# Feed-forward layer with seven block products for gate and up, and the weights' block sums on GpSimd

## The chip, the cores and the metric

The kernel runs on one core of a Trainium2 chip. The metric is the time of one execution on the device in microseconds (us); several executions are timed and their median is taken. The trace comes from one more execution, taken by the hardware profiler.

The engines in the text: TensorE (PE, with its weight loads PEld), VectorE (DVE), ScalarE (ACT), GpSimd (POOL) and SyncE (SP, which issues the loads).

## The reference

One inference step of a hybrid decoder layer for 512 prompt rows and 8 sample rows, so 520 columns in the transposed layout that the kernel uses. What matters here is the last step before the final norm, the feed-forward layer:

```
D_MODEL = 2048
D_FF = ((8 * D_MODEL + 3 * 256 - 1) // (3 * 256)) * 256

def channel_mix(x, lw):
    h = rms_norm(x, lw['g_ffn'])
    return x + (jax.nn.silu(h @ lw['w_gate']) * (h @ lw['w_up'])) @ lw['w_down']
```

D_FF is 5632. Everything is float32.

## The kernel before

The kernel is a sequence of stages (norm, input projection, RWKV, attention branches, output projection, feed-forward, final norm). Each stage is one block with an instruction list for each engine; the engines meet only at semaphores, and within one engine the instructions run in the order written. The change is in `stage_ffn`.

The residual `g.xt` lies in SBUF as 16 tiles of 128 x 520 (2048 features by 520 columns). The moving operands are halves of 260 columns (`HC`), each with a PSUM bank of its own. To reach float32 accuracy each product is made three times in the fast fp32r form: an operand is split into a rounded high part and the low remainder, and `three_products` adds high x high, high x low and low x high.

The loop runs over 11 rounds (`PARTS`), each for 512 of the 5632 hidden features. A round takes 12 weight tiles of 128 x 2048 (1 MB) in turn: gate and up for each of 4 hidden tiles, then 4 for the down projection. For tile n:

- SP loads it into one of 3 slots of `w_raw` (`load`, L2676 and L2680), when the tile that used the slot is finished;
- ScalarE rounds it to `w_hi` (`high`, L2751), VectorE subtracts to `w_lo` (`low`, L2779), both two tiles ahead of TensorE;
- TensorE multiplies: 16 x 6 = 96 matmuls of 260 columns for each gate or up tile, 4 x 2 x 2 x 6 = 96 for each down tile;
- VectorE scales the gate by the norm's factor (`gate`, L2785), ScalarE applies the Silu (L2760), GpSimd scales again (L2702), VectorE multiplies by up (`hidden`, L2791) and splits the result (L2793, L2795); for the down projection it adds the PSUM banks to the residual (`add`, L2803).

Norm: the factor 1/sqrt(mean square) of each column is not multiplied into the input but into gate and up afterwards, so that TensorE can begin as soon as the first input tile is scaled by the gain (ScalarE, L2764) and split (VectorE, L2823).

A line of `three_products` stands for matmuls of several stages; in the rows `d_ps<-hh` are gate and up, `d_ps<-f_hid_hi` is down. `three_products` is also used by the compression stage (`m_ps`), there with one output bank at a time. Rows of the RWKV preparation (`r_...`) show GpSimd and VectorE at work together.

Of the kernel before, what the change touches and what calls it, by code (L numbers as in the profile page):

```python
# [15 lines left out]
F32 = mybir.dt.float32  # L16
# [2132 lines left out]
def stage_nsa_prompt(nc, g):  # L2149
# [9 lines left out]
    with ExitStack() as ctx:  # L2159
# [28 lines left out]
        adr_in, late_in = sem("adr_in"), sem("late_in")  # L2188
# [310 lines left out]
def stage_out_proj(nc, g):  # L2499
    HC = TC // 2  # L2500
    with ExitStack() as ctx:
# [13 lines left out]
        with nc.Block() as block:  # L2515
# [10 lines left out]
            @block.gpsimd  # L2526
            def _(pool):
                for q in range(4, 8):
                    pool.wait_ge(mix_lo, q - 3)
                    mix_load(pool, g, q)  # L2530
# [101 lines left out]
def stage_ffn(nc, g):  # L2632
    HC = TC // 2
    HT = 4
    PARTS = D_FF // P // HT
    UN = 3 * HT
    SUMS = 16
    GR = 12
    assert PARTS * HT * P == D_FF and D == 2048
    with ExitStack() as ctx:  # L2640
        w_raw = g.wo_raw.rearrange("p s k n -> p s (k n)")
        w_hi = ctx.enter_context(nc.sbuf_tensor("f_w_hi", [P, 3, 2048], F32R))
        w_lo = ctx.enter_context(nc.sbuf_tensor("f_w_lo", [P, 3, 2048], F32R))
        hid_hi = ctx.enter_context(nc.sbuf_tensor("f_hid_hi", [P, HT, TC], F32R))
        hid_lo = ctx.enter_context(nc.sbuf_tensor("f_hid_lo", [P, HT, TC], F32R))
        spare = g.mix_raw.rearrange("p a b (h t) -> p a b h t", h=2)
        sg, act_up, rstd = spare[:, 0], spare[:, 1, 0], spare[:, 2]
        gain = ctx.enter_context(nc.sbuf_tensor("f_gain", [P, KT], F32))
        ps = g.ps_d
        loaded = [new_sem(nc, g, f"f_w_in{i}") for i in range(3)]  # L2650
        gain_in = new_sem(nc, g, "f_gain_in")
        hi_done, lo_done, summed, freed = (new_sem(nc, g, "f_" + n) for n in ("hi_done", "lo_done", "summed", "freed"))
        h_hi, h_lo, root_ready, rstd_ready = (new_sem(nc, g, "f_" + n) for n in ("h_hi", "h_lo", "root_ready", "rstd_ready"))
        gate_ready, silu_ready, gated, hid_split, hid_ready = (new_sem(nc, g, "f_" + n) for n in (
            "gate_ready", "silu_ready", "gated", "hid_split", "hid_ready"))
# [4 lines left out]
        def through(n):  # L2660

            return n + 1 if n < 2 * HT else 2 * HT + 2 * (n - 2 * HT) + 2

        def both(t):
            return t.rearrange("p (h t) -> p h t", h=2)

        with nc.Block() as block:
            @block.sync
            def _(sp):
                def load(i, n):  # L2670

                    i, n = (i, n) if n < UN else (i + 1, n - UN)
                    w = w_raw[:, n % 3, :]
                    if n < 2 * HT:
                        src = (gate_v, up_v)[n % 2][:, :, bass.ds(i * (HT * P) + (n // 2) * P, P)]
                        sp.dma_start(w.rearrange("p (k n) -> p k n", k=KT), src).then_inc(loaded[n % 3], 16)  # L2676
                    else:
                        v = n - 2 * HT
                        src = down_v[:, bass.ds(i * HT, HT), v * 512:(v + 1) * 512]
                        sp.dma_start(w.rearrange("p (k n) -> p k n", k=HT), src).then_inc(loaded[n % 3], 16)  # L2680

                def part(i, last):
                    for n in range(UN - 3 if last else UN):
                        sp.wait_ge(summed, i * SUMS + through(n))
                        load(i, n + 3)
                with nc.allow_non_contiguous_dma(reason="one value to a partition"):
                    sp.dma_start(gain[:], g.g_ffn.rearrange("(k p) -> p k", p=P)).then_inc(gain_in, 16)
                for n in range(3):
                    load(0, n)
                with sp.Fori(0, PARTS - 1) as i:  # L2690
                    part(i, False)
                part(PARTS - 1, True)

            @block.gpsimd
            def _(pool):
                clear_old(pool, g)
                pool.wait_ge(rstd_ready, 1)
                with pool.Fori(0, PARTS) as i:
                    for j in range(HT):
                        pool.wait_ge(silu_ready, i * HT + j + 1)  # L2700
                        take_wait(g, pool)
                        pool.tensor_tensor(sg[:, j % 2], sg[:, j % 2], rstd[:, 1], ALU.mult).then_inc(gated, 1)  # L2702

            @block.tensor
            def _(pe):
                def bank(group, j):
                    return ps[:, 4 * (group % 2) + j, 0:HC]

                def halves(x, k):
                    return [x[:, k, h * HC:(h + 1) * HC] for h in range(2)]  # L2710

                def part(i, first):
                    for n in range(2 * HT):
                        j, m, s = n // 2, n % 2, n % 3
                        pe.wait_ge(lo_done, i * UN + n + 1)
                        if m == 0:

                            pe.wait_ge(freed, i * GR + j + 1)
                        for k in range(KT):
                            if first and n == 0:  # L2720
                                pe.wait_ge(h_lo, k + 1)
                            cols = slice(k * P, (k + 1) * P)
                            last = three_products(pe, [bank(j, 2 * m + h) for h in range(2)], w_hi[:, s, cols], w_lo[:, s, cols],
                                                  halves(g.hh, k), halves(g.hl, k), k == 0, k == KT - 1)
                        last.then_inc(summed, 1)
                    for v in range(HT):
                        s = (2 * HT + v) % 3
                        pe.wait_ge(lo_done, i * UN + 2 * HT + v + 1)
                        for pair in range(2):
                            group = HT + 2 * v + pair  # L2730
                            pe.wait_ge(freed, i * GR + group + 1)

                            for ks in (range(HT - 1), range(HT - 1, HT)):
                                for m in range(2):
                                    for k in ks:
                                        if v + pair + m == 0:
                                            pe.wait_ge(hid_ready, i * HT + k + 1)
                                        c = k * 512 + (2 * pair + m) * P
                                        last = three_products(pe, [bank(group, 2 * m + h) for h in range(2)],
                                                              w_hi[:, s, c:c + P], w_lo[:, s, c:c + P],  # L2740
                                                              halves(hid_hi, k), halves(hid_lo, k), k == 0, k == HT - 1)
                            last.then_inc(summed, 1)
                for i in range(PARTS):
                    part(i, i == 0)

            @block.scalar
            def _(act):
                def high(i, n):
                    s = n % 3
                    act.wait_ge(loaded[s], i * (16 * UN // 3) + (n // 3 + 1) * 16)  # L2750
                    act.copy(w_hi[:, s, :], w_raw[:, s, :]).then_inc(hi_done, 1)  # L2751

                def part(i, last):
                    for n in range(UN):
                        if not last or n + 2 < UN:
                            high(i, n + 2)
                        if n < 2 * HT and n % 2 == 0:
                            j = n // 2
                            act.wait_ge(gate_ready, i * HT + j + 1)
                            act.activation(sg[:, j % 2], sg[:, j % 2], ACT.Silu).then_inc(silu_ready, 1)  # L2760

                act.wait_ge(gain_in, 16)
                for k in range(KT):
                    act.activation(g.hh[:, k, :], g.xt[:, k, :], ACT.Copy, scale=gain[:, k:k + 1]).then_inc(h_hi, 1)  # L2764
                    if k == 3:
                        high(0, 0)
                act.wait_ge(freed, 2)
                act.activation(rstd[:, 0], rstd[:, 0], ACT.Sqrt).then_inc(root_ready, 1)
                high(0, 1)
                with act.Fori(0, PARTS - 1) as i:  # L2770
# [4 lines left out]
            def _(dve):  # L2775
                def low(i, n):
                    s = n % 3
                    dve.wait_ge(hi_done, i * UN + n + 1)
                    dve.tensor_tensor(w_lo[:, s, :], w_raw[:, s, :], w_hi[:, s, :].bitcast(F32),  # L2779
                                      ALU.subtract).then_inc(lo_done, 1)  # L2780

                def gate(i, j):
                    dve.wait_ge(summed, i * SUMS + 2 * j + 1)
# [380 lines left out]
```

## Time and profile before

| | |
|---|---|
| median of 3 runs | 3720.39 us (3712.27 to 3722.6) |
| profiled execution | 3726.19 us, span 3724.6 us |
| TensorE's granted clock, mean | 0.939 |
| feed-forward stage | about 2158 to 3690 us of the span |
| weights loaded by the stage | 132 loads of 1 MB |
| matmuls of the stage | 12672 (8448 for gate and up, 4224 for down) |

The span runs from the first to the last instruction; the execution's time is a little more. A group of rows gives the line, engine, operation, out<-in, the shapes and the count; then busy time and the mean of one in ns; then the idle time of the engine just before them and what ended it. The matmuls are pipelined: one lasts 283 ns in the rows, but the next starts long before it ends.

### The profile page before, as it was taken

Reading aid. Unit: us, or ns where it says so; the run is one execution under the profiler, and the core shown is the slowest. Engines: PE = TensorE matmul, PEld = TensorE weight load, DVE = VectorE, ACT = ScalarE, POOL = GpSimd, SP = SyncE. Lnnn points to the kernel's source line nnn. Section 1 sums busy time; section 2 is a strip of 40 time slices with the busy share of each in tenths; the row PEclk is TensorE's granted clock in tenths of the full one; section 3 lists DMA queues with packets and bytes.
Section 4 is the critical chain, followed back from the end, with each engine's and each line's share of the span. In section 5 each row is a group of like instructions: output and inputs, shape, how many; then the busy total and the mean of one; then the engine's idle time right before and its main releaser. Section 6 shows DMA issues by size and latency. Waiting matters only on the chain. (4 is left out here: it accounts for less than half of the span.)

```text
span 3724.6 us, 67944 instructions
## 1 busy us (share of the span) xinstructions
PE 3379.1 (91%) x29423; PEld 3102.5 (83%) x29423; DVE 1407.2 (38%) x1761; ACT 1015.3 (27%) x1402; POOL 578.7 (16%) x697
## 2 busy tenths in 40 slices
PE   6999996769859999678779989999999999999997
PEld 6999996458837777454439989999999999999997
DVE  3222221833345665146633243333333333333334
ACT  4111111623215665134402132222122122122112
POOL 2000000534514333362000000000000000000000
PEclk8999998679979999769989999999999999999999
DMA  7433333455525442464143233233333233333332
GB/s 212 114 114 112 109 87 109 152 159 143 142 85 228 180 191 91 140 177 94 37 170 100 70 91 91 91 91 91 91 91 91 91 91 91 93 94 95 94 92 92
DMA packets 490816, 426.40 MB, mean 114 GB/s; under 512 B 124725, under 2 KB 439590, under 8 KB 485918
## 3 DMA queue, kind: packets, MB, share of 16 engines
q1 hardware_dynamic: 468222, 300.40, 28.8%
q0 software_dynamic: 20736, 122.13, 9.3%
q8 instruction: 214, 3.51, 0.4%
q14 instruction: 44, 0.36, 0.0%
q10 hardware_dynamic: 1600, 0.01, 0.0%
HBM read 382.99 MB, written 66.78 MB: 121 GB/s over the span
## 5 line engine op out<-in xcount | busy, mean ns | idle before, releaser
L2779 DVE TENSOR_TENSOR f_w_lo<-wo_raw,f_w_hi 128x2048 fp32r<-128x2048 f32 x132 | 302.5, 2292 | 813.1 <-ACT f_w_hi L2751 813.1
L53 PE MATMUL d_ps<-hh,f_w_hi 128*128 128x260 f32 x2816 | 567.6, 283 | 11.3 <-DVE f_w_lo L2779 11.3
L57 PE MATMUL d_ps<-hh,f_w_lo 128*128 128x260 f32 x2816 | 568.2, 283 | 0.0
L55 PE MATMUL d_ps<-hl,f_w_hi 128*128 128x260 f32 x2816 | 567.3, 283 | 0.0
L2751 ACT CAST f_w_hi<-wo_raw 128x2048 fp32r<-128x2048 f32 x132 | 252.1, 1910 | 998.1 <-DMA wo_raw<-in_w_gate 400.7
L53 PEld LDWEIGHTS d_ps<-hh,f_w_hi 128*128 128x128 f32 x2816 | 435.1, 189 | 11.9 <-DVE f_w_lo L2779 11.8
L57 PEld LDWEIGHTS d_ps<-hh,f_w_lo 128*128 128x128 f32 x2816 | 434.9, 189 | 0.0
L55 PEld LDWEIGHTS d_ps<-hl,f_w_hi 128*128 128x128 f32 x2816 | 433.6, 189 | 0.0
L53 PE MATMUL p_ps<-xh,p_w_hi 128*128 128x264 f32 (+2 forms) x1504 | 306.8, 285 | 10.8 <-DVE p_w_lo L306 10.8
L2702 POOL TENSOR_TENSOR mix_raw<-mix_raw 128x520 f32<-128x520 f32 x44 | 57.4, 1306 | 1621.7 <-ACT mix_raw L2760 1621.7
L55 PE MATMUL p_ps<-xl,p_w_hi 128*128 128x264 f32 (+2 forms) x1504 | 306.3, 285 | 0.0
L57 PE MATMUL p_ps<-xh,p_w_lo 128*128 128x264 f32 (+2 forms) x1504 | 305.6, 285 | 0.0
L53 PE MATMUL d_ps<-f_hid_hi,f_w_hi 128*128 128x260 f32 x1408 | 283.7, 283 | 1.2 <-DVE xt L2803 1.2
L57 PE MATMUL d_ps<-f_hid_hi,f_w_lo 128*128 128x260 f32 x1408 | 283.4, 283 | 0.0
L55 PE MATMUL d_ps<-f_hid_lo,f_w_hi 128*128 128x260 f32 x1408 | 282.4, 282 | 0.0
L53 PEld LDWEIGHTS p_ps<-xh,p_w_hi 128*128 128x128 f32 (+1 forms) x1504 | 232.8, 188 | 11.2 <-DVE p_w_lo L306 10.9
L55 PEld LDWEIGHTS p_ps<-xl,p_w_hi 128*128 128x128 f32 (+1 forms) x1504 | 232.9, 188 | 0.0
L57 PEld LDWEIGHTS p_ps<-xh,p_w_lo 128*128 128x128 f32 (+1 forms) x1504 | 232.6, 188 | 0.0
L1632 DVE TENSOR_TENSOR m_tb_lo<-m_ps,m_tb_hi 128x512 fp32r<-128x512 f32 (+1 forms) x272 | 169.2, 662 | 155.8 <-ACT m_tb_hi L1565 154.1
L53 PEld LDWEIGHTS d_ps<-f_hid_hi,f_w_hi 128*128 128x128 f32 x1408 | 217.6, 188 | 2.1 <-issue 1.9
L55 PEld LDWEIGHTS d_ps<-f_hid_lo,f_w_hi 128*128 128x128 f32 x1408 | 216.3, 188 | 0.0
L57 PEld LDWEIGHTS d_ps<-f_hid_hi,f_w_lo 128*128 128x128 f32 x1408 | 216.1, 188 | 0.0
(456 smaller groups left out, 5054.2 us busy)
## 6 DMA issues: line engine op xcount, KB each, us to landing
p_w<-in_w_in SPq DMA_DIRECT2D x46, 1024.0 KB, 5.6
wo_raw<-in_w_gate SPq DMA_DIRECT2D x44, 1024.0 KB, 5.6
wo_raw<-in_w_up SPq DMA_DIRECT2D x44, 1024.0 KB, 5.6
wo_raw<-in_w_down SPq DMA_DIRECT2D x44, 1024.0 KB, 5.1
wo_raw<-in_w_o SPq DMA_DIRECT2D x16, 1024.0 KB, 6.0
rk_chunks<-r_outb POOLq DMA_DIRECT2D x8, 1280.0 KB, 6.2
s_cur<-rk_chunks SPq DMA_DIRECT2D x8, 1280.0 KB, 7.2
s_one_vecs<-samp_rows SPq DMA_DIRECT2D x80, 128.0 KB, 4.7
```

The costliest lines, as they stand in the source:

```text
L53: pe.matmul(out[j], w_hi, x_hi[j], start=start, stop=False)
L55: pe.matmul(out[j], w_hi, x_lo[j], start=False, stop=False)
L57: last = pe.matmul(out[j], w_lo, x_hi[j], start=False, stop=stop)
L1632: dve.tensor_tensor(tb_lo[:, n % 4, 0:4 * w], ps[:, n % 4, 0:4 * w], tb_hi[:, n % 4, 0:4 * w].bitcast(F32), ALU.subtract).then_inc(dve_ev, 1)
L2702: pool.tensor_tensor(sg[:, j % 2], sg[:, j % 2], rstd[:, 1], ALU.mult).then_inc(gated, 1)
L2751: act.copy(w_hi[:, s, :], w_raw[:, s, :]).then_inc(hi_done, 1)
L2779: dve.tensor_tensor(w_lo[:, s, :], w_raw[:, s, :], w_hi[:, s, :].bitcast(F32), ALU.subtract).then_inc(lo_done, 1)
```

## The change

Gate and up are each computed by a Strassen-Winograd scheme with seven block products in place of eight. A round now makes 256 hidden features (22 rounds). The input is cut into 2 x 2 blocks (feature half by column half), the weights of a round likewise (feature half by hidden tile), each weight block 128 x 1024. The products are made in the order A11, S2, S3, S1, A12, S4, A22 (numbers 0 to 6 of gate, 7 to 13 of up), with

- S1 = A21 + A22, S2 = S1 - A11, S3 = A11 - A21, S4 = A12 - S2 of the weight blocks, made by GpSimd in every round (by VectorE only before the first gate);
- the like sums of the input blocks, made and split once before the loop (`t_f`, `t_hi`, `t_lo`), with the norm's factor and the gain multiplied in first;
- the four result quadrants put together by VectorE from the PSUM banks (`quarters`).

Each product is 8 x 3 = 24 matmuls into one bank. The down projection is 4 units of 48 matmuls a round (numbers 14 to 17), with two outputs of 24 each.

Weight loads are 512 KB, into six slots of `raw`; A21 lies in slot 1 and becomes S3 in place, and the low part also overwrites its raw block in place. Slots 0, 1, 4 and 5 serve the down projection too. So the low part of A11 waits until S3 has been made, and that of S2 until S4 has. The old weight and mixing buffers are released before the stage, and GpSimd clears one more list of semaphores at the start of the output projection.

The core of the diff (new lines of `stage_ffn`):

```diff
-    HT = 4
-    PARTS = D_FF // P // HT
-    UN = 3 * HT
...
+    KH = KT // 2
+    PARTS = D_FF // P // 2
+    PC = 7
+    DN = 4
+    W = 2 * PC + DN
+    GR = 2 * DN
...
+        A11, S2, S3, S1, A12, S4, A22 = range(PC)
+        LOADS = (3, 3, 1, 1, 2, 2)
+
+        def slot_of(n):
+
+            if n >= 2 * PC:
+                return (0, 1, 4, 5)[n - 2 * PC]
+            q, m = n // PC, n % PC
+            return {A11: 0, S3: 1, A12: 2 + 2 * q, A22: 3 + 2 * q}.get(m)
...
+        def add(eng, i, q, m):
+
+            count = (i * 2 + q) * 4
+            a11, a12, a21, a22 = (weights_f(q * PC + n) for n in (A11, A12, S3, A22))
+            x, y, op, needs = {
+                S1: (a21, a22, ALU.add, None),
+                S2: (weights_f(q * PC + S1), a11, ALU.subtract, count + 1),
+                S3: (a11, a21, ALU.subtract, None),
+                S4: (a12, weights_f(q * PC + S2), ALU.subtract, count + 2)}[m]
+            for n in {S1: (S3, A22), S2: (A11,), S4: (A12,)}.get(m, ()):
+                wait_loaded(eng, i, q * PC + n)
+            if needs is not None:
+                eng.wait_ge(added, needs)
+            eng.tensor_tensor(weights_f(q * PC + m), x, y, op).then_inc(added, 1)
```

On SP, the pairs are (products and units done before the load, what is loaded); W + ... is the next round:

```diff
+                def part(i, last):
+                    for done, n in ((1, PC + A11), (3, PC + S3), (5, W + A12), (7, W + A22), (8, 2 * PC), (10, 2 * PC + 1),
+                                    (12, 2 * PC + 2), (14, 2 * PC + 3), (15, W + A11), (16, W + S3),
+                                    (17, W + PC + A12), (18, W + PC + A22)):
+                        if not (last and n >= W):
+                            load(*(later(i, n) if n != W + A11 else (i, n)), i * W + done)
```

On GpSimd:

```diff
+                pool.wait_ge(scaled, 4)
+                pool.tensor_tensor(t_f[:, A12], t_f[:, A12], rstd[:, 0].unsqueeze(1).to_broadcast([P, KH, HC]),
+                                   ALU.mult).then_inc(pool_normed, 1)
+                pool.wait_ge(normed, 3)
+                pool.tensor_tensor(t_f[:, S3], t_f[:, S4], hid_f[:].rearrange("p v a h t -> p (v a h) t"),
+                                   ALU.subtract).then_inc(t3_made, 1)
+
+                def sums_of(i, q, done):
+
+                    part, lead = done
+                    pool.wait_ge(used, part * W + lead)
+                    for m in (S1, S2, S3):
+                        add(pool, i, q, m)
+                    pool.wait_ge(used, part * W + lead + 2)
+                    add(pool, i, q, S4)
+
+                pool.wait_ge(added, 4)
+                with pool.Fori(0, PARTS - 1) as i:
+                    sums_of(i, 1, (i, 4))
+                    sums_of(i + 1, 0, (i, PC + 4))
+                sums_of(PARTS - 1, 1, (PARTS - 1, 4))
```

On TensorE (`pair`, each product; `down`, each unit):

```diff
+                        for k in range(KH):
+                            w, wl, xh, xl = high_of(n)[:, k, :], weights(n)[:, k, :], t_hi[:, m, k, :], t_lo[:, m, k, :]
+                            pe.matmul(out, w, xh, start=(m < 4 and k == 0), stop=False, skip_group_check=True)
+                            pe.matmul(out, w, xl, start=False, stop=False, skip_group_check=True)
+                            last = pe.matmul(out, wl, xh, start=False, stop=(k == KH - 1), skip_group_check=True)
+                        last.then_inc(used, 1)
+
+                def down(i, c):
+                    n = 2 * PC + c
+                    pe.wait_ge(lo_done, i * W + n + 1)
+                    for e in range(2):
+                        d = 2 * c + e
+                        at = 4 * e
+                        if c:
+                            pe.wait_ge(freed, i * GR + d - 1)
+                        else:
+                            pe.wait_ge(c21_made, i * 2 + e + 1)
+                            pe.wait_ge(gate_freed, i + 1)
+                        for k, h in ((0, 0), (0, 1), (1, 1), (1, 0)):
+                            if d == 0 and h == k:
+                                pe.wait_ge(hid_ready, i * 3 + 2)
+                            if d == 0 and k > h:
+                                pe.wait_ge(hid_ready, i * 3 + 3)
...
+                        last.then_inc(used if e else half_done, 1)
```

On VectorE (`quarters` makes the quadrants and the product of gate and up; on ScalarE `high` waits for the load or the sum and for `used` as before):

```diff
+                def low(i, n):
+                    if n < 2 * PC and n % PC in (A11, S2):
+                        dve.wait_ge(added, (i * 2 + n // PC) * 4 + (3 if n % PC == A11 else 4))
+                    dve.wait_ge(hi_done, i * W + n + 1)
+                    dve.tensor_tensor(weights(n), weights_f(n), high_of(n).bitcast(F32), ALU.subtract).then_inc(lo_done, 1)
...
+                    if m == 6:
+                        if q:
+                            dve.tensor_tensor(u4, u2, ps[:, at + 3, 0:HC], ALU.add).then_inc(c12_made, 1)
+                            dve.wait_ge(c12_made, count)
+                            dve.tensor_tensor(h12, h12, u4, ALU.mult).then_inc(hid_made, 1)
...
+                def residual(i, d):
+                    if d % 2:
+                        dve.wait_ge(used, i * W + 2 * PC + d // 2 + 1)
+                    else:
+                        dve.wait_ge(half_done, i * DN + d // 2 + 1)
+                    at = 4 * (d % 2)
+                    x = g.xt[:, 2 * d:2 * d + 2, :].rearrange("p m (h t) -> p (m h) t", h=2)
+                    dve.tensor_tensor(x, x, ps[:, at:at + 4, 0:HC], ALU.add).then_inc(freed, 1)
...
+                    for n in range(W):
+                        q, m = n // PC, n % PC
+                        if q and m < 1:
+                            quarters(i, q - 1, PC)
+                        if n == 2 * PC:
+                            hidden_low(i, 2)
+                        if n > 2 * PC:
+                            residual(i, 2 * (n - 2 * PC) - 1)
+                        if q < 2:
+                            quarters(i, q, m)
+                        if not last or n + 2 < W:
+                            low(*later(i, n + 2))
+                        if n == 2 * PC - 1:
+                            hidden_low(i, 0)
+                            hidden_low(i, 1)
+                        if n >= 2 * PC:
+                            residual(i, 2 * (n - 2 * PC))
+                    residual(i, GR - 1)
...
+                scale(t(A11), 0, 1)
+                scale(b12, 1, 2)
+                dve.wait_ge(normed, 2)
+                dve.tensor_tensor(t(S1), b12, t(A11), ALU.subtract).then_inc(t_made, 1)
+                for m in (S1, S2, S3, S4):
+                    add(dve, 0, 0, m)
+                low(0, 0)
+                t_low(A11)
+                scale(t(S4), 1, 3)
+                dve.wait_ge(normed, 3)
+                dve.wait_ge(t_made, 1)
+                dve.tensor_tensor(t(S2), t(S4), t(S1), ALU.subtract).then_inc(t_made, 1)
+                dve.wait_ge(t_made, 2)
+                dve.wait_ge(pool_normed, 1)
+                dve.tensor_tensor(t(A22), t(A12), t(S2), ALU.subtract).then_inc(t_made, 1)
                 low(0, 1)
-                with dve.Fori(0, PARTS - 1) as i:
+                for m in range(1, PC):
+                    t_low(m)
+                part(0, False)
```

## Rows read from the trace of the kernel before

**Rows 1.** The page: busy time of each engine, share of the span, instructions.
```profile
PE 3379.1 (91%) x29423; PEld 3102.5 (83%) x29423; DVE 1407.2 (38%) x1761; ACT 1015.3 (27%) x1402; POOL 578.7 (16%) x697
```

**Rows 2.** Windows: busy PE, PEld, DVE, ACT, POOL; granted clock, DMA share, GB/s.
```profile
2190.00:3640.00 1450.00, 1448.79 (x12063) 1447.89 (x12063) 492.56 (x378) 290.50 (x187) 55.78 (x43) 1.00 0.32 92
```

**Rows 3.** Timeline of VectorE: the gate's first hidden tile in two successive rounds.
```profile
2321.55 0.70 DVE L2785 TENSOR_TENSOR mix_raw<-mix_raw,d_ps 128x520 f32<-128x520 f32 x1 [0.45 <-PE d_ps L57]
...
2460.83 0.69 DVE L2785 TENSOR_TENSOR mix_raw<-mix_raw,d_ps 128x520 f32<-128x520 f32 x1 [0.94 <-PE d_ps L57]
```

**Rows 4.** Waits of TensorE, 2170 to 3640 us: total, times, longest.
```profile
PE d_ps L53 <- DVE xt L2803: 1.2, 2, 0.7
```

**Rows 5.** Groups by line and shape, 2150 to 3640 us.
```profile
L2779 DVE TENSOR_TENSOR f_w_lo<-wo_raw,f_w_hi 128x2048 fp32r<-128x2048 f32 x129 | 295.6, 2292 | 795.4 <-ACT f_w_hi L2751 795.4
...
L2751 ACT CAST f_w_hi<-wo_raw 128x2048 fp32r<-128x2048 f32 x129 | 246.3, 1910 | 975.1 <-DMA wo_raw<-in_w_gate 400.7 <-DMA wo_raw<-in_w_down 330.0 <-DMA wo_raw<-in_w_up 244.3
...
L2803 DVE TENSOR_TENSOR xt<-xt,d_ps 128x1040 f32<-128x1040 f32 x80 | 98.5, 1234 | 26.9 <-PE d_ps L57 26.8
L2702 POOL TENSOR_TENSOR mix_raw<-mix_raw 128x520 f32<-128x520 f32 x44 | 57.4, 1306 | 1621.7 <-ACT mix_raw L2760 1621.7
L2785 DVE TENSOR_TENSOR mix_raw<-mix_raw,d_ps 128x520 f32<-128x520 f32 x44 | 30.6, 696 | 67.1 <-PE d_ps L57 67.1
...
L2760 ACT ACTIVATE mix_raw<-mix_raw 128x520 f32<-128x520 f32 x44 | 28.1, 639 | 190.1 <-DVE mix_raw L2785 190.1
```

**Rows 6.** Timeline of TensorE, compression stage: matmuls of a run of three into one bank.
```profile
1200.56 0.39 PE L53 MATMUL m_ps<-m_tb_hi,m_w_hi 128*128 128x512 f32 x1
1200.79 0.40 PE L55 MATMUL m_ps<-m_tb_lo,m_w_hi 128*128 128x512 f32 x1
```

**Rows 7.** Groups of GpSimd over the whole span.
```profile
L1141 POOL TENSOR_TENSOR s_one_t<-s_one_t 128x256 f32<-128x256 f32 x16 | 11.6, 726 | 1.3
```

**Rows 8.** DMA issues: count, KB each, median us from issue to landing.
```profile
mix_raw<-mix_t POOLq DMA_DIRECT2D x8, 520.0 KB, 5.2
...
kv_rows<-p_orow POOLq DMA_DIRECT2D x6, 512.0 KB, 3.4
...
mix_t<-a_mo POOLq DMA_DIRECT2D x4, 512.0 KB, 4.4
...
f_gain<-in_g_ffn SPq DMA_DIRECT2D x1, 8.0 KB, 3.0
```

**Rows 9.** Timeline of VectorE, RWKV preparation.
```profile
689.09 1.65 DVE L757 SCALAR_TENSOR_TENSOR r_kf<-r_kf,r_k_all 128x520 f32<-128x520 f32 x1
690.78 0.76 DVE L762 SCALAR_TENSOR_TENSOR r_rkk<-r_xr,r_vec,r_kf 128x520 f32<-128x520 f32 x1
...
692.06 0.69 DVE L773 TENSOR_TENSOR bonus_t<-r_xr,r_ps 128x520 f32<-128x520 f32 x1
...
695.31 1.76 DVE L785 SCALAR_TENSOR_TENSOR r_outb<-r_kkn,r_ex 128x512 f32<-128x512 f32 x1
```

**Rows 10.** Timeline of GpSimd in the same stretch.
```profile
688.77 1.42 POOL L568 TENSOR_TENSOR r_cum<-r_cum,r_sw 128x512 f32<-128x512 f32 x1 [1.43 <-DVE r_cum L753]
692.23 1.28 POOL L576 TENSOR_TENSOR r_bvec<-r_kkn,r_a 128x520 f32<-128x520 f32 x1 [2.04 <-DVE r_kkn L771]
...
694.68 0.62 POOL L582 COPY r_outb<-r_xr 128x512 f32<-128x512 f32 x1
695.26 1.26 POOL L583 TENSOR_TENSOR r_outb<-r_kf,r_ex 128x512 f32<-128x512 f32 x1
```

**Rows 11.** Timeline of TensorE and windows at the stage's start.
```profile
2155.27 2.79 PE L2538 MATMUL d_ps<-o_sq,ones 128*128 128x260 f32 x12
2169.34 0.80 PE L53 MATMUL d_ps<-hh,f_w_hi 128*128 128x260 f32 x2 [11.27 <-DVE f_w_lo L2779]
...
2155.00:2163.00 8.00, 3.07 (x16) 2.31 (x14) 2.23 (x5) 2.24 (x4) 0.00 (x0) 1.00 0.44 86
2163.00:2173.00 10.00, 3.67 (x17) 3.67 (x18) 8.02 (x10) 8.92 (x13) 0.00 (x0) 0.52 1.04 248
```

More of the change, by code:

```diff
@@ L2687, in _ @@
                     sp.dma_start(gain[:], g.g_ffn.rearrange("(k p) -> p k", p=P)).then_inc(gain_in, 16)
-                for n in range(3):
+                for n in (A11, S3, A22, A12, PC + A12, PC + A22):
                     load(0, n)
@@ L2712, in part @@
[L2712 to L2742, printed above, removed]
@@ new lines, in pair @@
+                def pair(i, q):
+                    at = 4 * q
+                    banks = {A11: at, A12: at, S2: at + 1, S3: at + 2, A22: at + 2, S1: at + 3, S4: at + 3}
+                    for m in range(PC):
+                        n = q * PC + m
+                        pe.wait_ge(lo_done, i * W + n + 1)
+                        if i == 0 and q == 0:
+                            pe.wait_ge(tl_done, m + 1)
+                        if m == 0 and i:
+                            pe.wait_ge(freed, i * GR + q - 1)
+                        if i == 0 and q == 1 and m == 0:
+                            pe.wait_ge(var_ready, 1)
+                        if m == A12:
+                            pe.wait_ge(p1_kept, i * 2 + q + 1)
+                        if m == S4:
+                            pe.wait_ge(u4_made, i * 2 + q + 1)
+                        if m == A22:
+                            pe.wait_ge(c22_made, i * 2 + q + 1)
+                        out = ps[:, banks[m], 0:HC]
+                        for k in range(KH):
[4 more added lines that the diff above has]
+                        last.then_inc(used, 1)
@@ L2743, in _ @@
                 for i in range(PARTS):
-                    part(i, i == 0)
+                    for q in range(2):
+                        pair(i, q)
+                    for c in range(DN):
+                        down(i, c)
             @block.scalar
@@ L2762, in _ @@
-                act.wait_ge(gain_in, 16)
-                for k in range(KT):
-                    act.activation(g.hh[:, k, :], g.xt[:, k, :], ACT.Copy, scale=gain[:, k:k + 1]).then_inc(h_hi, 1)
-                    if k == 3:
-                        high(0, 0)
[L2767 to L2770, printed above, removed]
+                    if slot_of(n) is None or n % PC == S3 and n < 2 * PC:
+                        q, m = n // PC, n % PC
+                        act.wait_ge(added, (i * 2 + q) * 4 + {S1: 1, S2: 2, S3: 3, S4: 4}[m])
+                    else:
+                        wait_loaded(act, i, n)
@@ new lines, in _ @@
+                act.wait_ge(gain_in, 16)
+                for n, (m, p, j) in enumerate(((A11, 0, 0), (None, 0, 1), (S4, 1, 1), (A12, 1, 0))):
+                    for k in range(KH):
+                        dst = hid_f[:].rearrange("p v a h t -> p (v a h) t")[:, k] if m is None else t_f[:, m, k]
+                        last = act.activation(dst, g.xt[:, p * KH + k, j * HC:(j + 1) * HC], ACT.Copy,
+                                              scale=gain[:, p * KH + k:p * KH + k + 1])
+                    last.then_inc(scaled, 1)
+                    if n == 1:
+                        high(0, 0)
@@ new lines, in _ @@
+                for m in range(PC):
+                    if m == A12:
+                        act.wait_ge(pool_normed, 1)
+                    elif m == S3:
+                        act.wait_ge(t3_made, 1)
+                    elif m in (A11, S4):
+                        act.wait_ge(normed, 1 if m == A11 else 3)
+                    else:
+                        act.wait_ge(t_made, {S1: 1, S2: 2, A22: 3}[m])
+                    act.copy(t_hi[:, m], t_f[:, m]).then_inc(th_done, 1)
+                    if m == 0:
+                        high(0, 1)
@@ new lines, in part @@
+                def part(i, last):
+                    for n in range(W):
+                        q, m = n // PC, n % PC
+                        if q and m < 1:
[4 more added lines that the diff above has]
+                            residual(i, 2 * (n - 2 * PC) - 1)
+                        if q < 2:
+                            quarters(i, q, m)
+                        if not last or n + 2 < W:
+                            low(*later(i, n + 2))
[5 more added lines that the diff above has]
+                    residual(i, GR - 1)
```

278 lines of the change are left out of this document (171 added, 107 removed).

## The prediction

> **What bounds the kernel now.** The page's busy times come first [rows 1]: TensorE is busy for 91% of the span, VectorE, the next, for 38%. The change sits in the feed-forward stage alone, so I read that stage. From 2190 to 3640 us TensorE is busy 1448.79 of 1450 us at the full granted clock [rows 2], and from 2170 on its waits add up to 1.2 us [rows 4]. The stage is TensorE's instruction stream: what shortens it shortens the kernel, and every microsecond in which TensorE waits is lost. The profiled execution took 3726.2 us with a span of 3724.6; the median of the three runs shown is 5.8 us lower (0.16%). I sum against 3726.2 and take 5.8 off at the end. A measurement of this kernel can tell about 0.3% (11 us) from no change.
>
> **What the change gives TensorE.** The same place in two rounds of the outer loop lies 139.28 us apart [rows 3]; a round has 1152 matmuls, so one takes 0.1209 us. Gate and up need 7392 matmuls where there were 8448, the down projection keeps its 4224: 1056 fewer, **-127.7 us**. One block product (24 matmuls) is then 2.90 us, one down unit (48) 5.80 us, and a new round 14 x 2.90 + 4 x 5.80 = 63.8 us. All 24 now go to one PSUM bank, where two banks alternated. Runs of three into one bank, 512 columns, start 0.23 us apart [rows 6], that is 0.45 ns a column against 0.46 here, so I charge nothing.
>
> **Prices of the new work.** VectorE from 0.696 us for 520 columns and 2.292 for 2048 [rows 5]: 1.22 us for 1024, 0.42 for 260, 2.33 for 2080; the residual add stays at 1.23. ScalarE from 0.639 and 1.910: 1.06 us for 1024, 1.94 for 2080. GpSimd from 0.726 us for 256 columns [rows 7] and 1.306 for 520 [rows 5], 2.20 ns a column: **2.41 us for a sum of 1024**, 4.74 for 2080. Loads are now 512 KB; transfers of 512 to 520 KB landed in 3.4, 4.4 and 5.2 us [rows 8], I take 4.2. A round has 8 sums, 19 us of GpSimd in 64; VectorE's work (18 low parts, 14 small adds and products, 3 splits, 8 residuals) is about 40 us. No engine passes TensorE by throughput. The latencies decide, because the sums form a chain in front of instructions that are queued in order.
>
> **Who holds whom.** While GpSimd subtracted from 688.77 to 690.19 [rows 10], VectorE's two-input instruction of 520 columns begun at 689.09 took 1.65 us, the like one after it 0.76 [rows 9]. The one at 695.31 took 1.76, beside a GpSimd product begun at 695.26. The one at 692.06, with one input in PSUM, took 0.69 beside GpSimd's product of 692.23. So a VectorE instruction with both inputs in SBUF stands until the running GpSimd instruction ends. GpSimd instructions that wait for nothing follow each other without a gap (0.62 us from 694.68, the next at 695.26). The low parts have both inputs in SBUF. The Trainium skill says the same ("SBUF - State Buffer", section "Who interferes with whom"): the shared pair is an exclusive lock, and who issues first blocks the other; the trace agrees, with 1.65 against 0.76 us. By that rule alone the sum behind S3, issued first, holds the low part up and the time is that of the forecast, 4023 us, not the first rival's 3905.
>
> **The end of a round.** The next round's S3 block is loaded into slot 1, which down unit 1 reads, so its load is queued on SP for the end of that unit; call it T. GpSimd's S1, S2 and S3 of the next gate all come after it, since S1 reads that block. The low part of the next A11 overwrites an operand of S3 and waits for it. On VectorE this low part stands ahead of residual 4, and TensorE needs residual 4 for output 6, the first half of down unit 3, due at T + 5.80. S4 waits for nothing by then and is queued directly behind S3, so it takes the lock before the low part. From T: load 4.2, four sums 9.64, low part 1.22, residual 1.23, hops 0.4 (SP, GpSimd, own semaphore): 16.7 us, a stall of **10.9 us**. Bounds: 10.1 and 11.9 by the load; 2.4 less if the low part slips in ahead of S4. What is late next, the low part of S2, still ends before its product. After an idle 11.27 us before this stage TensorE came back at half clock (0.52 granted from 2163 to 2173, 17 matmuls in 3.67 us) [rows 11]: 0.216 us each against 0.121, 1.6 us, and some 0.2 beyond that window. I add **1.8 us**. 21 round ends: 21 x 12.7 = **+267 us**.
>
> **The middle of a round.** For up, the S3 block is loaded when product 2 is done (8.7 us into the round) and lands at 13.1. The low part of product 6 runs from 12.75 to 13.97 and holds S1 back. From 13.97: four sums 9.64, own semaphore 0.1, low part of A11 1.22: product 7 can begin at 25.0, due at 20.3. **4.7 us**, 22 times: +103. Bounds: 2.3 if the low part beats S4, 1.1 if nothing blocks at all; 5 with a slow load. Whether the clock falls in so short a gap no row here tells; 0 to 1.8 us, I take 0.5 (in the 11.27 us gap, begun at 2158.06, it still stood at 1.00 up to 2163) [rows 11]: +11.
>
> **The hidden values.** Behind product 12 stand on VectorE an add and a product (0.84), a low part (1.22, after ScalarE's 1.06), and splits of 260 and 520 columns (1.12): 3.4 us with hops against the 2.9 of product 13. 0.7 x 22 = **+15** (bounds 0 and 33). The remaining quadrant has the first 2.2 us of down unit 0 as cover.
>
> **The start.** Before, TensorE began 10.9 us after the stage (2169.34 against some 2158.4, where the stage begins) [rows 11], because the split could follow the gain tile by tile. Now ScalarE makes 32 scaled half tiles of about 0.43 us once the gain has landed (3.0 us) [rows 8], then a high part and the copy of A11 (to 19.8). VectorE follows with the low part of A11, three more block operations, one weight part, six low parts and the low part of weight 2: ten of 2.33 and two of 1.22, to 45.6, and two GpSimd operations of 4.74 with the lock push it to 45.6 to 55. TensorE has done two products by then and goes on at about 50, where 5.8 would have been due; its cold start it paid before as well. 50 - 5.8 - 10.9 = **+34** (28 to 40).
>
> The loads (same bytes), the table loads of the Silu (1.3 us, ScalarE is half idle), and the extra semaphore clears on GpSimd in front of its loads of the output projection, which wait for VectorE there, cost nothing. The sum: -127.7 + 267 + 103 + 11 + 15 + 34 = +302; 3726.2 + 302 - 5.8 = **4023 us**.
>
> **Rivals.**
> *The low part slips in ahead of S4* (chance 0.22). VectorE starts within hundredths of its semaphore, and if S4 takes the lock later than that, both stalls shrink by 2.4: -127.7 + 21 x 10.3 + 22 x 2.3 + 15 + 30 = +184, **3905 us**. Against it: GpSimd's next record begins before the last one ends [rows 10].
> *The sums stay covered* (0.05): one mechanism, the A11 low part at the end of the round not holding residual 4 up, and product 7 finding its sums made. Then -127.7 + 15 + 34 = -79, **3642 us**. It decides from where the two stalls together, clock included, fall under 3.5 us a round (79 / 22). For it: GpSimd is idle two thirds of the time. Against: the shortest load (3.4), three sums, a low part and a residual make 13.1 us where 5.8 are there.
> *A block product costs more than its columns* (0.05): with 24 matmuls into one bank 0.01 us dearer each, 11616 x 0.01 = +116 on top, **4139 us**. Against it stand the runs of three [rows 6].
> *The change doesn't thin out the matmuls* I give nothing: their count is fixed by the loops.
>
> **How the numbers follow.** My forecast, S4 ahead of the low part, gets 0.66; the rest, 0.02, is a sum that happens to cancel. All cases but one are slower. Its own bounds: loads of 3.4 us, no clock loss in the middle and the shortest start give 4023 - 17 - 11 - 6 = 3989; loads of 5.2, a cold clock after both stalls and the longest start give 4023 + 21 + 7 + 29 + 6, 4086. The range reaches down to the first rival less its own slack, 3885, and up to 4100. Faster by over 0.3%: 0.05; within: 0.02; slower: 0.93.
>
> **What would show it.** In the profile after: about 11616 matmuls in the stage at 0.12 us; rounds of some 83 us instead of 63.8; TensorE's longest waits for the residual add, about 11 us, 21 times, and for the low part in the middle, about 4.7 us, 22 times; a half clock after the former; GpSimd's 1024-column sums at 2.4 us, S4 directly behind S3; low parts of 1.2 us that show 3.6 beside S4. The forecast is wrong if loads land in 3 us or less, if GpSimd's sums are much faster than 2.4 us, or if S4 leaves VectorE a gap.

## The result, and the profile after

| | before | after |
|---|---|---|
| median | 3718.91 us (4 runs) | 4061.33 us (4058.21 to 4064.34, 4 runs) |
| ratio | | 1.0923 (95% interval 1.0904 to 1.0942) |
| profiled execution | 3726.19 us, span 3724.6 | 4058.21 us, span 4056.2 |
| mean granted clock | 0.939 | 0.897 |

The change makes the kernel 9% slower. The forecast was 4023 us, the range 3885 to 4100.

The page of the changed kernel, busy time of each engine (answers to [rows 1]); TensorE has 1056 matmuls fewer, and is busy for 83% of the span in place of 91%:

```profile
PE 3358.6 (83%) x28367; PEld 3073.9 (76%) x28367; DVE 1849.2 (46%) x2312; ACT 1208.2 (30%) x1824; POOL 955.6 (24%) x827
```

Windows of the loop, 2260 to 4020 us (columns as in [rows 2]), and TensorE's waits from 2170 us on (answers to [rows 4]): what it waited for, total, times, longest.

```profile
2260.00:4020.00 1760.00, 1445.39 (x11118) 1433.39 (x11118) 890.06 (x904) 459.77 (x566) 413.00 (x168) 0.90 0.25 75
```

```profile
PE d_ps L2838 <- DVE xt L2991: 215.0, 21, 11.1
PE d_ps L2814 <- DVE f_raw_r L2939: 98.8, 23, 6.8
PE d_ps L2814 <- DVE f_t_lo_r L3027: 36.0, 2, 26.9
PE d_ps L2838 <- DVE f_hid_r L2982: 11.8, 21, 0.6
```

Before, the stage had 1.2 us of waits. Now there is one wait of some 10.2 us for the residual add at each of 21 round ends; one for the low part of A11 in each of 22 rounds (98.8 less the 6.8 of the start, 4.2 each); 43 us at the start (36.0 and 6.8); and 0.6 a round for the hidden values. The granted clock over the loop is 0.90, where it was 1.00 [rows 2].

One round end shows the whole chain. GpSimd's and VectorE's timelines:

```profile
3015.26 2.37 POOL L2730 TENSOR_TENSOR f_sums<-f_raw 128x1024 f32<-128x1024 f32 x1 [40.84 <-DMA f_raw<-in_w_gate]
3017.71 2.34 POOL L2730 TENSOR_TENSOR f_sums<-f_sums,f_raw 128x1024 f32<-128x1024 f32 x1
3020.00 2.35 POOL L2730 TENSOR_TENSOR f_raw<-f_raw 128x1024 f32<-128x1024 f32 x1
3022.30 2.34 POOL L2730 TENSOR_TENSOR f_sums<-f_raw,f_sums 128x1024 f32<-128x1024 f32 x1
3048.57 3.29 POOL L2730 TENSOR_TENSOR f_sums<-f_raw 128x1024 f32<-128x1024 f32 x1 [23.92 <-DMA f_raw<-in_w_up]
```

```profile
3011.19 1.24 DVE L2991 TENSOR_TENSOR xt<-xt,d_ps 128x1040 f32<-128x1040 f32 x1 [1.65 <-PE d_ps L2842]
3022.48 3.25 DVE L2939 TENSOR_TENSOR f_raw_r<-f_raw,f_w_hi 128x1024 fp32r<-128x1024 f32 x1 [10.05 <-POOL f_raw L2730]
3025.65 2.37 DVE L2991 TENSOR_TENSOR xt<-xt,d_ps 128x1040 f32<-128x1040 f32 x2
...
3048.38 1.23 DVE L2939 TENSOR_TENSOR f_raw_r<-f_raw,f_w_hi 128x1024 fp32r<-128x1024 f32 x1 [0.20 <-ACT f_w_hi L2862]
3056.80 3.25 DVE L2939 TENSOR_TENSOR f_raw_r<-f_raw,f_w_hi 128x1024 fp32r<-128x1024 f32 x1 [7.20 <-POOL f_raw L2730]
```

Residual 3 begins at 3011.19, when down unit 1 ends. GpSimd sits idle 40.84 us until the gate's block has landed, 4.1 us after that. S1, S2, S3 (which writes `f_raw`) and S4 follow, 2.35 us each. VectorE has waited 10.05 us for S3; its low part of A11 begins at 3022.48, 0.18 us after S4, and takes 3.25 us where others take 1.23. Only then come residuals 4 and 5, which were ready long before. In the middle of the round it is the other way about once: S1 begins 0.19 us after a low part and takes 3.29.

TensorE's timeline at that round end and at the next middle:

```profile
3027.02 0.56 PE L2838 MATMUL d_ps<-f_hid_r,f_w_hi 128*128 128x260 f32 x1 [10.10 <-DVE xt L2991]
```

```profile
3055.53 0.28 PE L2815 MATMUL d_ps<-f_t_lo_r,f_w_hi 128*128 128x260 f32 x1
3055.65 0.28 PE L2816 MATMUL d_ps<-f_t_hi,f_raw_r 128*128 128x260 f32 x1
3060.11 0.49 PE L2814 MATMUL d_ps<-f_t_hi,f_w_hi 128*128 128x260 f32 x1 [4.18 <-DVE f_raw_r L2939]
...
3062.78 0.42 PE L2814 MATMUL d_ps<-f_t_hi,f_w_hi 128*128 128x260 f32 x1
3062.99 0.42 PE L2815 MATMUL d_ps<-f_t_lo_r,f_w_hi 128*128 128x260 f32 x1
```

Ahead of a gap matmuls start 0.12 us apart, all into one bank; behind it 0.21 to 0.22, the 1.2 GHz level. In the round shown that lasted for 27 matmuls behind the 10 us gap and for 16 behind the 4 us gap. One round doesn't stand for all: behind the 4 us gap of the round before, at 2975.55, it lasted for 28. Windows behind the 4 us gaps at 2975.55 and 3060.11 (columns as in [rows 2]):

```profile
2975.80:2981.70 5.90, 5.90 (x28) 5.90 (x29) 2.68 (x4) 2.33 (x4) 0.00 (x0) 0.50 0.01 3
3060.40:3063.50 3.10, 3.10 (x16) 3.10 (x16) 2.64 (x3) 1.78 (x3) 0.00 (x0) 0.50 0.02 5
```

Over the loop the rounds alternate between the two kinds. Counted from the start times of all its matmuls, 17 to 27 run at half clock behind the long gap (22.5 on average, 2.3 us lost) and 13 to 28 behind the short one (21.5, 2.2 us lost). The two gaps cost nearly the same.

Groups of the stage (answers to [rows 5]) and loads (answers to [rows 8]):

```profile
L2939 DVE TENSOR_TENSOR f_raw_r<-f_raw,f_w_hi 128x1024 fp32r<-128x1024 f32 x264 | 410.5, 1555 | 425.0 <-POOL f_raw L2730 372.3 <-ACT f_w_hi L2862 50.4
...
L2939 DVE TENSOR_TENSOR f_sums_r<-f_sums,f_w_hi 128x1024 fp32r<-128x1024 f32 x132 | 161.2, 1221 | 181.3 <-ACT f_w_hi L2862 181.3
...
L2730 POOL TENSOR_TENSOR f_raw<-f_raw 128x1024 f32<-128x1024 f32 x43 | 101.9, 2369 | 0.0
```

```profile
f_raw<-in_w_gate SPq DMA_DIRECT2D x88, 512.0 KB, 3.9
```

The mean low part from `f_raw`, 1555 ns, hides two kinds: 43 of 3.25 us and the others of 1.23.

### The profile page after: what moved, and what is told of

It reads as the page before. It is cut to its first block and busy times, and to the rows that moved or that the text cites. A ratio compares the mean times of both kernels' runs of the same rounds, so it can differ in the third digit from the quotient of the medians.

```text
span 4056.2 us, 69046 instructions
## 1 busy us (share of the span) xinstructions
PE 3358.6 (83%) x28367; PEld 3073.9 (76%) x28367; DVE 1849.2 (46%) x2312; ACT 1208.2 (30%) x1824; POOL 955.6 (24%) x827
## 5 line engine op out<-in xcount | busy, mean ns | idle before, releaser
L2814 PE MATMUL d_ps<-f_t_hi,f_w_hi 128*128 128x260 f32 x2464 | 725.0, 294 | 134.8 <-DVE f_raw_r L2939 98.8
L2815 PE MATMUL d_ps<-f_t_lo_r,f_w_hi 128*128 128x260 f32 x2464 | 721.8, 293 | 0.0
L2838 PE MATMUL d_ps<-f_hid_r,f_w_hi 128*128 128x260 f32 x1408 | 423.9, 301 | 227.4 <-DVE xt L2991 215.0
L2939 DVE TENSOR_TENSOR f_raw_r<-f_raw,f_w_hi 128x1024 fp32r<-128x1024 f32 x264 | 410.5, 1555 | 425.0 <-POOL f_raw L2730 372.3
L2814 PEld LDWEIGHTS d_ps<-f_t_hi,f_w_hi 128*128 128x128 f32 x2464 | 489.5, 199 | 140.3 <-DVE f_raw_r L2939 103.7
L2815 PEld LDWEIGHTS d_ps<-f_t_lo_r,f_w_hi 128*128 128x128 f32 x2464 | 488.8, 198 | 0.0
L2838 PEld LDWEIGHTS d_ps<-f_hid_r,f_w_hi 128*128 128x128 f32 x1408 | 288.0, 205 | 235.2 <-issue 235.2
L2840 PE MATMUL d_ps<-f_hid_r,f_w_hi 128*128 128x260 f32 x1408 | 419.6, 298 | 0.0
L2816 PE MATMUL d_ps<-f_t_hi,f_raw_r 128*128 128x260 f32 x1408 | 419.2, 298 | 0.0
L2842 PE MATMUL d_ps<-f_hid_r,f_raw_r 128*128 128x260 f32 x1408 | 418.6, 297 | 0.0
L53 PE MATMUL p_ps<-xh,p_w_hi 128*128 128x264 f32 (+2 forms) x1504 | 306.7, 285 | 10.9 <-DVE p_w_lo L306 10.9
L2816 PE MATMUL d_ps<-f_t_hi,f_sums_r 128*128 128x260 f32 x1056 | 299.9, 284 | 0.0
L2840 PEld LDWEIGHTS d_ps<-f_hid_r,f_w_hi 128*128 128x128 f32 x1408 | 288.2, 205 | 0.0
```

The lines of the kernel that those rows point to most:

```text
L53: pe.matmul(out[j], w_hi, x_hi[j], start=start, stop=False)
L2814: pe.matmul(out, w, xh, start=(m < 4 and k == 0), stop=False, skip_group_check=True)
L2815: pe.matmul(out, w, xl, start=False, stop=False, skip_group_check=True)
L2816: last = pe.matmul(out, wl, xh, start=False, stop=(k == KH - 1), skip_group_check=True)
L2838: pe.matmul(out, high_of(n)[:, k, cols], hid_hi[:, k, h, :], start=(k == 0), stop=False, skip_group_check=True)
L2840: pe.matmul(out, high_of(n)[:, k, cols], hid_lo[:, k, h, :], start=False, stop=False, skip_group_check=True)
```

## The experiments

All are edits of the changed kernel. Ratios are to the kernel before, timed again beside them: 3723.75 us beside the first three, 3721.34 us beside the others. So differences of a few us between the two groups say nothing.

**S4 after the low part of A11.** GpSimd waits with S4 until VectorE is done with that low part.

```diff
                     pool.wait_ge(used, part * W + lead + 2)
+                    pool.wait_ge(lo_done, i * W + q * PC + A11 + 1)
                     add(pool, i, q, S4)
```

> Edit: GpSimd makes S4 only when the low part of A11 of the same matrix is done, so that S4 doesn't take the lock ahead of it. My theory: the low part takes 1.2 us in place of 3.25 beside S4; both stalls shrink by 2.1 to 2.3 us, in the middle of the round some 0.8 us come back because S4 and the low part of S2 now follow each other; 4061 - 21 x 2.2 - 22 x 1.4 = about 3984 us, 40 us more gained if the clock holds in the shorter gaps. Rival (no lock; the 3.25 us of the low part are a wait for something else, such as ScalarE's rounded part): no gain, 4040 to 4075 us.

Measured: 3950.61 us, ratio 1.0613 (1.0594 to 1.0633), 111 us less than the changed kernel. TensorE's waits from 2260 us on:

```profile
PE d_ps L2839 <- DVE xt L2992: 170.3, 21, 8.8
PE d_ps L2815 <- DVE f_raw_r L2940: 44.8, 21, 2.7
```

VectorE at a round end (timeline), and GpSimd beside it:

```profile
3052.63 1.23 DVE L2940 TENSOR_TENSOR f_raw_r<-f_raw,f_w_hi 128x1024 fp32r<-128x1024 f32 x1 [10.07 <-POOL f_raw L2730]
```

```profile
3054.02 2.36 POOL L2730 TENSOR_TENSOR f_sums<-f_raw,f_sums 128x1024 f32<-128x1024 f32 x1 [1.51 <-DVE f_raw_r L2940]
```

The low part is back at 1.23 us: the lock is real, and worth 2.1 us in each of the two places (10.2 to 8.1 and 4.2 to 2.1). Those are some 88 us of waiting. The expectation allowed 77, with 0.8 us coming back for S2 that didn't come back, and up to 40 more for the clock. Counted from the matmuls' start times in the two traces, the half clock cost 21 us less.

**VectorE makes all sums.** In place of GpSimd, right before the low parts that wait for them; GpSimd's loop of sums is taken out (not shown).

```diff
...
                 def low(i, n):
+                    if n < 2 * PC and n % PC in (A11, S2) and (not isinstance(i, int) or i or n >= PC):
+                        q = n // PC
+                        for m in (S1, S2, S3) if n % PC == A11 else (S4,):
+                            add(dve, i, q, m)
```

> Edit: VectorE makes all weight sums, right before the low parts that wait for them, in place of GpSimd; loads, slots and the order of the other VectorE work stay. My theory: a sum takes 1.22 us, there is no S4 in front and no lock; in the middle of a round the low part ends about 19 us into the round, before it is due at 20.3, so that stall (4.2 us and 1.6 of half clock) goes; at the end the load stays late: 4.2 + 3 sums 3.7 + low part 1.2 + residual 1.2 + hops 0.3 = 10.6 against 5.8, a stall of 4.8 in place of 10.2. 4061 - 22 x 5.8 - 21 x 6.3 = about 3800 us, still slower than the kernel before. Rival (GpSimd's pace is the whole cause): both stalls go, 4061 - 22 x 5.8 - 21 x 12.5 = about 3670 us, faster than before.

Measured: 3805.85 us, ratio 1.0228 (1.0202 to 1.0253). The waits from 2260 us on:

```profile
PE d_ps L2823 <- DVE xt L2980: 98.3, 21, 5.7
PE d_ps L2823 <- DVE f_hid_r L2971: 11.8, 21, 0.6
```

The wait in the middle is gone, the one at the end is 4.7 us, as worked out. So another engine for the sums gives back 256 us, with every load where it was, and the kernel is still slower than before: the late load is a cause of its own.

**Residuals first.** On VectorE, residuals 4, 5 and 6 go ahead of the low part of the next A11.

```diff
+                        if n == W - 2:
+                            residual(i, GR - 4)
+                            continue
+                        if n == W - 1:
+                            residual(i, GR - 2)
+                            if not last:
+                                low(*later(i, W))
                         if not last or n + 2 < W:
                             low(*later(i, n + 2))
+                        if n == W - 1:
+                            continue
```

> Edit: VectorE adds residuals 4, 5 and 6 ahead of the low part of the next round's A11; GpSimd, loads and slots stay. My theory: the residual no longer holds output 6 up; TensorE finishes the round and waits only for the low part itself, which ends some 15 us after down unit 1 where the next round is due at 11.6: a stall of about 3.5 us in place of 10.2, now with the low part as its end, and 1 us less half clock: 4061 - 21 x 7.7 = about 3900 us. Rival (the chain of load, sums and low part bounds the round, the residual is only where the wait shows): the wait moves whole to the next product, 4030 us or more.

Measured: 3904.81 us, ratio 1.0494 (1.0461 to 1.0527). The waits from 2260 us on:

```profile
PE d_ps L2814 <- DVE f_raw_r L2939: 158.4, 42, 5.0
PE d_ps L2838 <- DVE f_hid_r L2982: 11.8, 21, 0.6
```

No wait for a residual is left. Of the 42 waits for a low part half are those of the middle (4.2 us, 88 together), the other 70 us are the round end's, 3.4 each. The queue order alone cost 6.8 us a round: residual 4 needs nothing of what it stood behind.

**The S3 block loaded early.** Down unit 1 reads slot 2 in place of slot 1. The next S3 block is then loaded after product 9; the late place falls to the A12 block, which of the four sums only S4 needs.

```diff
-        LOADS = (3, 3, 1, 1, 2, 2)
+        LOADS = (3, 2, 2, 1, 2, 2)
...
-                return (0, 1, 4, 5)[n - 2 * PC]
+                return (0, 2, 4, 5)[n - 2 * PC]
...
-                    for done, n in ((1, PC + A11), (3, PC + S3), (5, W + A12), (7, W + A22), (8, 2 * PC), (10, 2 * PC + 1),
-                                    (12, 2 * PC + 2), (14, 2 * PC + 3), (15, W + A11), (16, W + S3),
+                    for done, n in ((1, PC + A11), (3, PC + S3), (7, W + A22), (8, 2 * PC), (9, 2 * PC + 1), (10, W + S3),
+                                    (12, 2 * PC + 2), (14, 2 * PC + 3), (15, W + A11), (16, W + A12),
```

> Edit: down unit 1 reads slot 2 in place of slot 1 (its load follows that of unit 0), so the next round's S3 block is loaded right after product 9 and the next A12 block takes the late place. GpSimd still makes every sum. My theory (the late load of the S3 block starts the chain that holds residual 4 up): S1 runs early, S2 and S3 follow the A11 block that lands about 4 us after down unit 0, S4 waits for its A12 block and so doesn't stand in front of the low part; the wait for the residual falls from 10.2 us to under 1 us, and with some 2 us of half clock behind it goes about 21 x 12 = 250 us: about 3815 us. The 4.2 us in the middle of a round stay. Rival (the sums on GpSimd and their lock on VectorE cost the time, wherever the load lies): most of the stall stays, over 3960 us.

Measured: 3809.88 us, ratio 1.0237 (1.022 to 1.0255), 251 us less than the changed kernel. The waits from 2260 us on, and GpSimd's timeline over a round end:

```profile
PE d_ps L2814 <- DVE f_raw_r L2939: 86.2, 21, 4.2
...
PE d_ps L2838 <- DVE xt L2991: 4.5, 3, 3.7
```

```profile
3029.41 3.41 POOL L2730 TENSOR_TENSOR f_sums<-f_raw 128x1024 f32<-128x1024 f32 x1 [16.75 <-DMA f_raw<-in_w_gate]
3048.36 2.40 POOL L2730 TENSOR_TENSOR f_sums<-f_sums,f_raw 128x1024 f32<-128x1024 f32 x1 [15.54 <-DMA f_raw<-in_w_gate]
```

S1 is made 19 us before S2, and the wait for the residual falls from 215.0 to 4.5 us, with every sum still on GpSimd. The stall in the middle stays as it was (4.1 us a round).

**Both, all sums on VectorE.** The slots of the run before and VectorE's sums (the two diffs above).

> Edit: the slots of the run before and VectorE making every sum. My theory: the 4.7 us at the end of a round, left with VectorE's sums, go with the early load, and what is left of the loss is the start and the hidden values: 3806 - 98 - about 25 of half clock = some 3680 us, 1% faster than the kernel before. Rival (the end of the round is bound by VectorE's own queue, with sums and low parts ahead of the residuals): at least half of the 4.7 us stay, 3730 us or more.

Measured: 3694.93 us, ratio 0.9925 (0.9908 to 0.9941). The waits for the residual from 2145 us on:

```profile
PE d_ps L2823 <- DVE xt L2980: 35.2, 21, 1.7
```

Between the two: 0.75% faster than before, but 15 us over the expectation. 1.7 us a round end stay. VectorE's timeline shows why:

```profile
3056.34 1.24 DVE L2980 TENSOR_TENSOR xt<-xt,d_ps 128x1040 f32<-128x1040 f32 x1 [1.65 <-PE d_ps L2827]
3057.50 1.22 DVE L2730 TENSOR_TENSOR f_sums<-f_raw 128x1024 f32<-128x1024 f32 x1
...
3061.24 1.23 DVE L2928 TENSOR_TENSOR f_raw_r<-f_raw,f_w_hi 128x1024 fp32r<-128x1024 f32 x1
3062.38 2.38 DVE L2980 TENSOR_TENSOR xt<-xt,d_ps 128x1040 f32<-128x1040 f32 x2
```

S1 follows residual 3 at once, without a wait for a load. Residual 3, three sums and the low part fill 6.0 us before residual 4 can begin, and that add takes 1.2 more, where down unit 2 gives 5.8 of cover. That is the rival's mechanism, VectorE's own queue, at 1.7 us in place of the half of 4.7 or more that it allowed. The gains of the two edits are not to be added: 251 and 256 us by themselves, 366 together, because the stall at the round end shrinks with either.

**Both, the sums divided.** The same slots; GpSimd makes the gate's sums at the round end, VectorE those of up (the condition in `low` begins with `PC <= n < 2 * PC`).

```diff
-                pool.wait_ge(added, 4)
                 with pool.Fori(0, PARTS - 1) as i:
-                    sums_of(i, 1, (i, 4))
                     sums_of(i + 1, 0, (i, PC + 4))
-                sums_of(PARTS - 1, 1, (PARTS - 1, 4))
```

> Edit: the same slots; GpSimd makes the gate's sums at the end of a round, VectorE those of up in the middle. My theory: with the S3 block loaded early GpSimd's sums have cover at the end of a round, and the lock costs VectorE only time that it has: the same as with VectorE making all of them, within 15 us, some 3680 us. Rival (any sum on GpSimd holds low parts or residuals up for TensorE): 3715 us or more.

Measured: 3659.5 us, ratio 0.9831 (0.9815 to 0.9848): 1.7% faster than before and with the next one the fastest, 21 us under the expectation and 35 us under all sums on VectorE. The loop's window and the waits from 2145 us on:

```profile
2260.00:3630.00 1370.00, 1350.74 (x11125) 1344.65 (x11124) 937.10 (x989) 461.36 (x567) 213.35 (x83) 1.00 0.31 96
```

```profile
PE d_ps L2811 <- DVE f_t_lo_r L3028: 36.0, 2, 26.9
PE d_ps L2835 <- DVE f_hid_r L2983: 15.6, 22, 0.8
PE d_ps L2811 <- DVE f_raw_r L2940: 7.1, 1, 7.1
PE d_ps L2835 <- DVE xt L2992: 4.2, 2, 3.7
```

The loop runs at the full clock, and a round takes 64.7 us (TensorE's wait for the hidden values ends at 3033.07 and at 3097.78), where 63.6 are matmuls (528 at 0.1205). Of the 35.2 us of waits for the residual 4.2 are left. GpSimd's sums cost TensorE next to nothing where they have cover.

**A shorter start.** As the run before, with weights 2 and 3 prepared between the splits of the input blocks (VectorE's part; `high` on ScalarE is moved likewise, and the first round leaves out what is done already).

```diff
...
                 for m in range(1, PC):
                     t_low(m)
+                    if m in (2, 3):
+                        low(0, m)
```

> Edit: as the run before, and in the first round the rounded and low parts of weights 2 and 3 are made between the splits of the input blocks, right behind those of blocks 2 and 3, and not behind all seven. My theory: product 2 begins some 8 us earlier, the later ones follow the splits, and the start is 5 to 10 us shorter: about 3672 us. Rival (product 4 waits for the end of the splits whatever comes before it): no change, within 3 us of the run before.

Measured: 3660.93 us, ratio 0.983 (0.9812 to 0.9848), no change that these runs can tell, as the rival has it. In the profile the wait of 7.1 us for weight 2 is gone, but product 4 now waits for its low part, which stands behind the last splits:

```profile
2210.02 0.39 PE L2811 MATMUL d_ps<-f_t_hi,f_w_hi 128*128 128x260 f32 x1 [3.65 <-DVE f_raw_r L2942]
```

The 36.0 us for the splits of the first two blocks stay. Counted from the begin of the stage, product 2 comes 7.0 us earlier and the second round 4.2 us earlier, less than single executions differ by. The expectation of 5 to 10 us was too high.

## Why the prediction was right, point by point

- *The matmuls.* Right. The new count is there, and 24 into one bank cost no more: 0.12 us each.
- *The end of a round*, forecast 10.9 us of stall: 10.2. In the round shown the load and its hand-over to GpSimd took 4.07 us, the four sums 9.38 (9.64 in the forecast's sum), the low part 1.09 behind S4, the residual and TensorE's restart 1.29: 15.83 where that sum had 16.7. The first rival falls: S4's record begins 0.18 us before the low part's, and taking S4 out of its way gave 2.1 us. The load's place, the pace of the sums, S4 and the order of low part and residual were each changed in a run of its own, and the waits moved about as the sum has it: from 10.2 us a round to 0.2, 4.7, 8.1 and 3.4.
- *The middle of a round*, forecast 4.7: 4.2. The load doesn't set the length here: it lands while the low part of product 6 runs, and S1 stands behind that, as charged. The difference lies in four sums of 9.4 us in place of 9.64 and a low part that ended 1.1 us behind S4 in place of 1.22.
- *The clock* is the term that was mis-sized. Behind the round end I charged 1.8 us, measured are 2.3 (22.5 matmuls at some 0.22 us in place of 0.12); for the middle I took 0.5 between 0 and 1.8, measured are 2.2, above that range. Together 4.5 us a round where I had 2.3, some 47 us in all.
- *The round.* Forecast 82.4 us; S1 of the gate comes at 2262.73 and, 20 rounds on, at 3935.65, so 83.65 us. From the start times of the matmuls: 528 at 0.1205 are 63.6; the three gaps, from one start to the next and less an ordinary step, are 10.4, 4.3 and 0.7; the half clock is 4.5. Together 83.5, and nothing of size is left over. (The profile's waits are some 0.2 us shorter than these gaps, since they count from the modelled end of the matmul before.)
- *The start*, +34: product 2 begins at 2203.69, 53.4 us after the stage (2150.31); by the same working +36.7. GpSimd's two large operations held VectorE up as charged: a sum of 1.22 took 5.60 us there and a difference of 2.33 took 6.60.
- *The hidden values*, 0.7: 0.6.
- *The sum.* 4061 is 38 us over the forecast: the clock gives +47, the start and the hidden values +5, the shorter stalls -18 (0.5 and 0.4 a round, as gaps from start to start), 34 together; the rest is no more than single executions differ by. That the forecast came within 1% is in part luck: the stalls were taken too long and the clock's share too small.
- *The sums stay covered* (the rival on the other side) fell for the changed kernel; with the slots changed and half of the sums on VectorE both stalls are gone but for 4.2 us, and 3659.5 us stand beside the 3642 worked out for it.

But for the extra semaphore clears on GpSimd the work ahead of the stage is unchanged, yet the stage began between 2147.6 and 2158.4 us in the nine profiled executions: of a difference of 10 us between two single profiles nothing is to be concluded.

## What to carry to other kernels

When work moves to a slower engine that is idle most of the time, compare chains and not sums of busy time: from the event that lets it begin (here the release of a slot and a 4 us load) through its instructions to the instruction that waits, and then look at what is queued behind the waiting one. A slot shared with the last work of a round sets when the next round's first chain can start; giving the late place to the block that the sums need last was worth 251 us, as much as the choice of the engine (256 us with the late load, 115 with the early one), and with it the slower engine was even the better place for half of the sums, by 35 us. With fewer matmuls the gaps must not come in their place: beside its length a gap here cost matmuls at half clock, 2.3 us on average behind one of 10.2 and nearly as much, 2.2, behind one of 4.2.

## What the runs showed of the hardware that was not expected

A gap as short as 2.1 us also brought the half clock. In the run with S4 after the low part TensorE waited 2.13 us before 3085.42, ran nine matmuls, eight of them 0.12 us apart, and then fell to the 1.2 GHz level for 16, until 3090 (granted clock 0.52 from 3086.50 to 3090.00):

```profile
3085.42 0.39 PE L2815 MATMUL d_ps<-f_t_hi,f_w_hi 128*128 128x260 f32 x1 [2.13 <-DVE f_raw_r L2940]
...
3086.37 0.28 PE L2816 MATMUL d_ps<-f_t_lo_r,f_w_hi 128*128 128x260 f32 x1
3086.49 0.31 PE L2817 MATMUL d_ps<-f_t_hi,f_raw_r 128*128 128x260 f32 x1
...
3087.03 0.42 PE L2817 MATMUL d_ps<-f_t_hi,f_raw_r 128*128 128x260 f32 x1
3087.25 0.42 PE L2815 MATMUL d_ps<-f_t_hi,f_w_hi 128*128 128x260 f32 x1
```

All 21 such gaps of that run were followed by this, at 1.6 us each. The 21 waits of 1.7 us at the round ends of the run with both edits and all sums on VectorE were not: but for the first step the matmuls went on 0.12 us apart behind them, and the granted clock was 1.00 over the loop.

The lock goes by who comes first, in both directions: a low part 0.18 us behind S4 waited two microseconds (3.25 in place of 1.23), and S1 0.19 us behind a low part waited one (3.29 in place of 2.37).
